# Router logits taken from the centred residual, and eleven cached pages loaded during the third tile of the time mixer

## The reference, cut to what matters

```
x = layer_norm(ALPHA * x + mixer(x), ln1_g, ln1_b)
lc = x @ moe_w_coarse + moe_b_coarse          # 4 groups
lf = x @ moe_w_fine[g] + moe_b_fine[g]        # 4 experts of each group
group = argmax(lc); two best experts of that group; weights by softmax
x = layer_norm(ALPHA * x + sum of the two experts, ln2_g, ln2_b)

layer_norm(x, g, b) = (x - mean) * rsqrt(var + 1e-5) * g + b
sample attention: softmax(q . cache_kv[page] + q_rope . cache_krope[page]) over 8 pages of 128 positions per sample
```

## Time and profile before

| what | value |
|---|---|
| three runs | 956.81, 960.07, 961.41 us, median 960.07 |
| profiled execution | 960.22 us, of which the span from the first to the last instruction is 958.5 |
| PE busy | 858.3 us, 90% of the span |
| DVE, ACT, POOL busy | 436.3, 244.0, 165.2 us |
| mean granted TensorE clock | 0.904 of full speed |
| DMA | 165.25 MB, 172 GB/s mean |

### The profile page before, as it was taken

The page is one execution under the profiler, slowest core; times in us unless marked ns, Lnnn a source line. Parts: engine busy times, 40 slices in busy tenths (PEclk is TensorE's granted clock), DMA queues, the critical chain, the costliest instruction groups (busy, mean ns, idle before and its releaser), DMA issues.

```text
span 958.5 us, 20599 instructions
## 1 busy us (share of the span) xinstructions
PE 858.3 (90%) x8552; PEld 616.0 (64%) x8552; DVE 436.3 (46%) x965; ACT 244.0 (25%) x532; POOL 165.2 (17%) x217
## 2 busy tenths in 40 slices
PE   5999998979999998999789889788978969999995
PEld 3787776757466656877655756558755747566653
DVE  3599754653124235148723343423634354042435
ACT  1135212051111113165235122130650060101013
POOL 5106041001400001000069630000810002300000
PEclk9999979998899999999999686865989988999997
DMA  9764802263999995421010220000826354999901
GB/s 263 258 176 75 162 12 94 89 234 102 413 417 416 418 307 159 132 75 63 1 19 4 90 79 4 2 1 3 252 89 220 132 224 166 417 417 417 415 36 46
DMA packets 79835, 165.25 MB, mean 172 GB/s; under 512 B 19809, under 2 KB 58136, under 8 KB 70850
## 3 DMA queue, kind: packets, MB, share of 16 engines
q1 hardware_dynamic: 68348, 149.43, 43.6%
q0 software_dynamic: 6624, 14.06, 4.9%
q10 hardware_dynamic: 4768, 0.41, 0.5%
HBM read 155.70 MB, written 6.99 MB: 170 GB/s over the span
## 4 chain that ended last, share of the span: by engine, by line
PE 76%; DVE 12%; issue 5%; ACT 2%; SPq 2%; DMA 2%; POOLq 0%; POOL 0%; DVEq 0%; ACTq 0%
PE bank L1666 12%; PE bank L2078 12%; PE bank L2110 7%; PE bank L1948 6%; PE bank L2122 5%; PE bank L816 3%; DVE scratch L2196 3%; PE bank L670 2%; SPq L2891 1%; PE bank L2067 1%; PE bank L694 1%; PE bank L2057 1%; DVE scratch L2193 1%; PE bank L2046 1%; PE bank L684 1%
## 5 line engine op out<-in xcount | busy, mean ns | idle before, releaser
L2651 ACT ACTIVATE scratch<-bank 128x280 f32<-128x280 f32 (+5 forms) x122 | 57.2, 476 | 415.9 <-PE bank L2110 114.2
L1666 PE MATMUL bank<-x_fm,weight_slots 128*128 128x280 f32 x576 | 142.7, 409 | 2.7 <-ACT x_fm L2742 1.3
L1666 PEld LDWEIGHTS bank<-x_fm,weight_slots 128*128 128x128 f32 x576 | 111.8, 195 | 31.5 <-issue 3.5
L2078 PE MATMUL bank<-weight_slots,scratch 128*64 128x256 f32 x672 | 92.5, 379 | 0.0
L2196 DVE TENSOR_TENSOR scratch<-bank,scratch 128x256 f32<-128x256 f32 x16 | 6.8, 425 | 157.4 <-PE bank L2078 157.4
L2078 PEld LDWEIGHTS bank<-weight_slots,scratch 128*64 128x64 f32 x672 | 58.6, 137 | 26.2 <-issue 4.6
L2122 PE MATMUL bank<-scratch 128*128 128x280 f32 x256 | 66.6, 406 | 0.0
L2196 DVE TENSOR_TENSOR scratch<-scratch 128x128 f32<-128x128 f32 (+14 forms) x76 | 50.8, 682 | 30.5 <-ACT scratch L2651 28.5
L1948 PE MATMUL bank<-scratch,weight_slots 128*128 128x280 f32 x256 | 62.6, 402 | 0.0
L1948 PEld LDWEIGHTS bank<-scratch,weight_slots 128*128 128x128 f32 x256 | 48.1, 190 | 13.7 <-issue 1.7
L2078 PE MATMUL bank<-scratch 128*64 128x256 f32 x352 | 56.9, 379 | 0.0
(11 more groups left out here) (441 smaller groups left out, 1308.6 us busy)
## 6 DMA issues: line engine op xcount, KB each, us to landing
weight_slots<-in_moe_w_down SPq DMA_DIRECT2D x24, 1024.0 KB, 12.6
weight_slots<-in_moe_w_up SPq DMA_DIRECT2D x22, 1024.0 KB, 10.7
weight_slots<-in_moe_w_gate SPq DMA_DIRECT2D x20, 1024.0 KB, 11.0
scratch<-in_moe_w_gate SPq DMA_DIRECT2D x12, 1024.0 KB, 9.9
scratch<-in_moe_w_up SPq DMA_DIRECT2D x10, 1024.0 KB, 10.7
weight_slots<-in_od_w_in SPq DMA_DIRECT2D x9, 1024.0 KB, 6.3
weight_slots<-in_ev_w_in SPq DMA_DIRECT2D x8, 1024.0 KB, 14.7
scratch<-in_moe_w_down SPq DMA_DIRECT2D x8, 1024.0 KB, 12.7
```

The lines of the kernel that those rows point to most:

```text
L1666: ins = pe.matmul(b[:, 0:NT], w[:, k, P * m2:P * m2 + P], src[:, k, :], start=(k == 0), stop=(k == kt - 1))
L2078: ins = pe.matmul(b[CAP * j:CAP * j + CAP, 0:DE], XG[:, q % 2, k, CAP * j:CAP * j + CAP], w[j][:, k, :], start=(k == 0), stop=(k == KD - 1))
L2651: return act.activation(dst, b[:rows, 0:width], f, **kw).then_inc(ring.free, 1)
```

## The change

Two things that don't touch each other, and a few small helpers.

First, the logits no longer come from the normed `XT`. With c the centred residual, s the scale of a token, g and b the norm's weight and bias and W the router's weights, x @ W = s * (c @ (g * W)) + b @ W. So the 16 x 20 columns of router weights are multiplied by `ln1_g` once, b @ W is added once to `RB`, both for both layers and ahead of layer 0's norm (on PE 32 one-column matmuls, counted as two per product by the profile, and two 20-column ones; on ACT three small activations and one copy; on DVE one multiply of 128x320 and one add of 128x40). In each layer the eight router matmuls now read `RES` right behind the squares, their bank is in ring A, ACT copies it to `LG4`, and DVE multiplies it by the spread scale ahead of the eight tiles of `RES`. The turn to token-major follows the scale. ACT now does all eight tiles of layer norm 1 (`ACT_TILES = (KD, 6)`; six still in layer norm 2), and all three `x_turned` come behind the logits, once all eight tiles of `XT` are there.

Second, of the 47 late pages, eleven have their homes in what the time mixer calls `ATF`, `KTF` and `BTF`, and these wait for `mark["rbk"]` of the third tile (DVE's last read of the products in which these tiles were used) in place of `y_free` = 3.

```diff
-EARLY_PAGES, READY_PAGES = 17, 56
+EARLY_PAGES, MIDDLE_PAGES, READY_PAGES = 17, 11, 56
-ACT_TILES = 6
+ACT_TILES = (KD, 6)
+        free_middle = [(16800 + 4 * 288, MIDDLE_PAGES)]
-        free_late = [(1024, 8), (5600, 11), (9248, 7), (16800, 16), (25152, 5)]
+        free_late = [(1024, 8), (5600, 11), (9248, 7), (16800, 4), (16800 + 15 * 288, 1), (25152, 5)]
...
                 if n == EARLY_PAGES:
...
+                    sp.wait_ge(*mark["rbk"])        # the same on POOL
+                if n == EARLY_PAGES + MIDDLE_PAGES:
                     sp.wait_ge(y_free, len(PT))
...
# PE, once, between hn_mean and hn_var; BC, BCB, RBX are new small tiles
+            for l in range(2):
+                for k in range(KD):
+                    g, w0 = 32 * (k % 4), 20 * (KD * l + k)
+                    ins = pe.matmul(b[g:g + 32, l:l + 1], RWF[:, w0:w0 + 32], vec("ln1_b", KD * l + k), start=(k < 4), stop=(k >= 4))
+            close(A, ins, "router_bias")
# behind hn_var
+            until("router_bias")
+                ins = pe.matmul(b[:, 20 * l:20 * l + 20], BCB[:, l, :], cst("sum4"), start=True, stop=True)
+            close(A, ins, "router_rows")
...
# PE, each layer
-                spread_scale(2 * l)
-                b = V.claim()
+                b = A.claim()
                 for k in range(KD):
-                    ln_tile(2 * l, k)
+                    if k < KD - 1:
+                        pe.wait_ge(ev("ln_centred"), (KD - 1) * 2 * l + k + 1)
+                    else:
+                        until(f"out{l}")
-                    ins = pe.matmul(b[g:g + 32, 0:NT], RWF[:, w0:w0 + 32], XT[:, k, :], start=(k < 4), stop=(k >= 4))
-                close(V, ins, f"lg{l}")
+                    ins = pe.matmul(b[g:g + 32, 0:NT], RWF[:, w0:w0 + 32], RES[:, k, :], start=(k < 4), stop=(k >= 4))
+                close(A, ins, f"lg{l}")
+                spread_scale(2 * l)
...
-                x_turned(0)
-                until(f"lg{l}")
+                pe.wait_ge(ev("lg_scaled"), l + 1)
                 # 3 small matmuls: sum4 of LG4
-                x_turned(1)
-                x_turned(2)
+                for k in range(KD):
+                    ln_tile(2 * l, k)
+                for t in range(3):
+                    x_turned(t)
...
# DVE, scaled(c)
                 b = V.take()
+                if c % 2 == 0:
+                    until(f"lg{c // 2}")
+                    s.mark(mul(LG4, LG4, b[:, 0:NT]), ev("lg_scaled"))
                 for m in range(KD):
                     s.mark(mul(RES[:, m, :], RES[:, m, :], b[:, 0:NT]), ev("ln_scaled"))
-                for m in range(ACT_TILES, KD):
+                for m in range(ACT_TILES[c % 2], KD):
...
# DVE, out_and_moe(l)
+                if l == 0:
+                    until("router_rows")
+                    s.do(mul(rw, rw, bc(vec("ln1_g", 0, 2 * KD), [P, 2 * KD, 20], 2)))
+                    s.do(add(RB[:, :, :], RB[:, :, :], RBX))
-                scaled(2 * l)
                 s.mark(dve.memset(PICK, 0.0), dve_step)
                 s.do(dve.memset(LG, 0.0))
-                s.do(dve.tensor_copy(LG4, b[:, 0:NT]), v_free)
+                scaled(2 * l)
...
# ACT, layer_norm, behind the root
+                if c % 2 == 0:
+                    empty(LG4, NT)
-                for m in range(ACT_TILES):
+                for m in range(ACT_TILES[c % 2]):
```

More of the change, by code:

```diff
@@ L367, in program @@
         MEANQ = part(5840, NT)
+        BC, BCB, RBX = part(4780, 2), part(4784, 2, P), part(5040, 2, 20)
         x_loads = [
@@ L440, in rows_landed, with tiles_of @@
             return 16 * sum((m, k) <= (l, q) for m in range(2) for k in range(1, NQ) if k % 4 == q % 4)
+        def tiles_of(c):
+            return sum(ACT_TILES[i % 2] for i in range(c))
         kt_read, score_banks = {}, {}
@@ L1897, in _ @@
             close(A, ins, "hn_var")
+            until("router_bias")
+            b = A.claim()
+            for l in range(2):
+                ins = pe.matmul(b[:, 20 * l:20 * l + 20], BCB[:, l, :], cst("sum4"), start=True, stop=True)
+            close(A, ins, "router_rows")
             def spread_norms():
                 pe.wait_ge(ev("norm_scale"), 1)
+                pe.wait_ge(a_free, A.n)
                 norms.extend((A.n, A.slot))
@@ L2212, in _ @@
             v2 = lambda r: r.rearrange("p (a b) -> p a b", a=2)
[L2213 removed]
+            s.do(mul(v2(t0), v2(are), dt), ev("angles"))
             s.do(mul(v2(t1), v2(aim), dt))
@@ L2720, in std @@
                     empty(sd[:, m, :], NT, ACT.Sqrt, scale=1.0 / n, bias=eps[e])
+            b = A.take()
+            s.do(act.activation(BC, b[:, 0:2], ACT.Copy))
+            s.do(act.activation(BCB[:, 0, :], cst("ones"), ACT.Identity, scale=BC[:, 0:1]))
+            act.activation(BCB[:, 1, :], cst("ones"), ACT.Identity, scale=BC[:, 1:2]).then_inc(a_free, 1)
             empty(OSD[:, 0, :], NT, ACT.Sqrt, scale=32.0 * 32.0 / RDV, bias=eps["32 1e-5"])
+            empty(RBX.rearrange("p l e -> p (l e)"), 40)
             for h in range(RH):
```

39 lines of the change are left out of this document (19 added, 20 removed).

## The result

| | before | after |
|---|---|---|
| median of the runs | 961.03 us (8 runs, 956.81 to 965.47) | 952.09 us (8 runs, 949.07 to 957.15) |
| profiled execution | 960.22, span 958.5 | 957.15, span 955.4 |
| mean granted clock in it | 0.904 | 0.896 |

After / before is 0.9919, with a 95% interval of 0.9891 to 0.9946: 7.8 us less, between 5.2 and 10.5 (the two medians lie 8.9 apart). The forecast was 953.4. The profiled execution of the changed kernel is the slowest of its eight, so the two profiles differ by 3.1 us only. They have to be compared stage by stage, not by their spans.

A forecast was written before the change was run, and what follows sets the result against it. TensorE, busy 90% of the span, was taken to bound the kernel through its work, gaps and clock. From 960.2, pages -6.0, router -1.2 and front +0.4 gave 953.4 us, range 949.2 to 957.3.

The forecast's parts named there:

- Part 1: Late pages of layer 1's mixer: eleven loaded during the third tile save 6.0 us, bounds 4.0 and 6.3.
- what is late next is ACT: After the third tile, PE next waits for ACT's exponentials, done at 704.5; the earlier start gains 4.0 us.
- I take 'stays': Clock stays up over PE's remaining 2.2 us wait before the probabilities' turns, bringing 2.0 us more.
- Rival (b): Clock falls in the 2.2 us wait left by ACT, router gives between nothing and 1.2: 956.0 us, chance 0.25.
- Rival (c): Pages do nothing, because something other than POOL's pace sets the last landing: 959.4 us, chance 0.06.
- Part 2: Router logits taken early in both layers' norm 1: 1.2 us saved over two layers, bounds 0 and 5.5.
- So I take half clock: After 4.0 us of idle PE, the router stage's 24 turns run at half clock, taking 5.2 us.
- ACT is not in the way: Router stage: ACT finishes its exponential and three small copies at 217.9, before `PLACE` wants them.
- 0.6 us of 0.9: Packing after the router: of 0.9 us earlier `PLACE`, 0.6 survives per layer, depending on when the clock returns.
- rival (d): The new 4.0 us gap holds the clock down past packing, 3.7 us lost per layer: 964.0 us, chance 0.05.
- Part 3: One-time router preparation ahead of layer 0's norm costs 0.4 us, bounds 0 and +1.5.
- The clock is full here: Ahead of layer 0's projection, full clock lets the two 20-column products cost only 0.4 us.

The follow-up runs named there:

- The router alone: Section on the change with all 47 pages late again, 958.28 us; its four: that, the change, and the change with idle products at the front or second weighing.
- pages_only: The kernel before plus only the eleven pages loaded in the third tile, old router kept: 956.02 us, ratio 0.9968.
- five_pages: The kernel before plus only five of the eleven pages loaded in the third tile, old router kept: 955.45 us, ratio 0.9954.
- orders_fed_two: both_orders plus three idle TensorE products ahead of the front's variance sums and three ahead of the second page weighing: 940.00 us, ratio 0.9812.
- both_orders: The change with ACT's three PICK copies ahead of its exponential and table load, and half the turns ahead of the second four tiles: 949.76 us, ratio 0.9885.

## Why the prediction came out right, point by point

**Part 1, the pages: right in mechanism, the size somewhat high.** The step "the wait goes entirely" and "what is late next is ACT" is what the earlier trace rows's counterpart shows: 2.13 us idle, released by the accumulation at L1483, where 2.2 was forecast. "I take 'stays'" was right for this gap in this profile (PEclk 1.00 from 707 to 712; 24 scores in 2.78 us). Rival (b)'s reason, that nothing on record keeps the clock over a gap of this length, had a counterexample in the prediction's own: 2.04 us, followed by 16 products in 4.04 us at a granted clock of 1.00. Between this pair of profiles the stage gave 5.87 us, forecast 6.0. On the means of all profiles it gave 4.5: the wait for the landing is 4.7 us in the two others that have it, and the clock stood at half behind it for 3.4 us there, not 6.8. So the 2.0 us which the forecast put on the clock were read off an execution in which it cost more than in the others. 4.5 is still within the bounds that the prediction gave. Rival (c) is out: the longest landing was 4.3 us and nobody waits for one.

**Part 2, the router: -1.2 was forecast, half in each layer. The means show 2.0 us gained in layer 0 up to the slots and nothing in layer 1.**
- The bias is added, and the routing walk on DVE starts, 2.7 us earlier after the root: right.
- "So I take half clock" for the turns was right for the start of them only. They took 4.40 us, not 5.2, as the clock came back inside them, at 214.6. "The counting of tokens ran at half already and still does" was wrong: it ran at full clock, and PE was done at 218.0, which is 216.0 with the 2.0 us of the later start taken off, against the 219.0 forecast. By the rule of the Trainium skill that the prediction cited (TensorE: Matmul & The Clock Gate, "Part 4: PE-mode transpose"), the fast clock doesn't engage in transposes. Here it came back after PE had done nothing but turns for 3.2 us and nothing at all for 4.0 us before them, and the kernel with idle products ahead of the turns ran all 24 at 1.00 in 2.78 us. The measurement decides: the rule doesn't hold for these float32 turns.
- "ACT is not in the way" was wrong, though ACT's own time was right. With the 2.0 us of the later start taken off, its copies end at 219.88 - 2.0 = 217.9, the number forecast; but as PE came earlier than forecast, ACT became the last. Putting the copies first moved `PLACE` by 1.5 and 1.8 us, which shows it. So `PLACE` gained 1.88 and 1.67, not 0.9.
- "0.6 us of 0.9" for the packing and what follows was the mis-sized step in layer 1. PE now idles before the packing for 3.7 us (1.88 before, at a clock that was at half anyway; both from layer 0). From `PLACE` to the slots the four profiles with the new router that are named under "The router alone" have 0.6 to 0.7 us more on the means than the four with the old one, from the slots to the end 1.3 more (162.0 to 162.3 against 160.7 to 160.8 us), and the expert loop's first 34 us stand at 0.85 in place of 0.90. That is the mechanism of rival (d), a clock held down past the packing, at less than half of its price: layer 1's net is 0, where -0.6 was forecast. In layer 0 the packing of the change ran 6.6 us at half in place of 3.5, but pages_only, with the old router, took 9.34 us there as well, and what happens behind the slots drowns in the 440 us stretch.

**Part 3, the front: the work was sized right, the clock was left out, and at 2.14 us the stage lies outside the bounds of 0 and +1.5.** The one-column products (32 by the profile's count) took 0.43 us inside the gap, and the small ones 0.62 against 0.4 forecast. The other 1.7 us of the 2.14 come from a clock that falls at about 167 and makes the projection's start 5.71 us in place of 4.02. "The clock is full here" was read off one profile of the kernel before, and another with the old router (five_pages) has the same fall. Idle products in the gap took 1.69 of the 2.14 away, at a clock of 1.00, which shows that it is the clock; the 0.45 that stays is the added work. Against the mean of the three profiles with the old router and the gap left empty (37.0 us) the front costs 1.6 us and not 2.14.

**The sum.** On the means of the stages the change is worth -4.5 (pages) - 2.0 (router, layer 0) + 0 (router, layer 1) + 1.6 (front) = -4.9 us, an estimate; from the one pair of profiles it is -5.9 + 2.1 - 0.5 + 0 = -4.3. The parts measured alone agree with the means: the pages 3.1 and 4.4 us, the router 1.2, and the product 0.9968 x 0.9988 = 0.9956 is 4.2 us. The change itself measured 7.8 us, with 5.2 as its lower end; by the intervals of the two parts I estimate that their product is good to about 4 us either way, so the two are not clear of each other. The forecast of -6.8 lies between, and its closeness owes something to chance: the pages and the front came out 1.5 and 1.2 us worse than forecast, the router 0.8 better. Where the other 3 us of the 7.8 come from, if they are more than noise, is not settled: no stage that the diff touches shows them, and the stretch of 440 us between varies by more than that from one execution to the next. Likewise open is why the two orders with two filled gaps gain 5 to 6 us more than the expected sum of their stages. That the clock stands at half for less of the time would fit both (the mean granted clock was 0.909 to 0.913 in all six runs of orders_fed_two, 0.900 to 0.903 in those of both_orders), but a profile shows one execution, of the others only the mean clock is known, and no run changes the middle stretch alone.

## What to carry to other kernels

A wait that is removed brings what lies between it and the next engine's readiness: find who is late next before you move more than is needed (five pages did nearly what eleven did). Take the length of a stage from several profiles: one pair gave the pages 5.9 us, the means 4.5. A dependency that is taken away early can leave PE idle later, and here a longer gap in front of the turns and the packing was followed by a lower clock, and in layer 1 all that the earlier start had gained was gone by the end, so the layer's time from a fixed landmark to its end is the number to look at, and not the landmark in between. Where PE has gaps of some 2 us amid light work, a few idle products on constants are a cheap trial: in two places, with an order that shortens the other gaps, they took the kernel with both orders from 0.9885 to 0.9812.

## What was not expected of the hardware

- The clock fell after a short gap with little work in it: the gap of the earlier trace rows (2.04 us), with 32 one-column products in it and 4 small ones behind it (the profile's count), was followed by a granted clock of 0.50 from 167 on (5.71 us for 16 products against 4.02), and the stage was as long in all seven profiles that had them with the gap left empty; without them it was 2.1 us shorter in two profiles of three, and the third had the fall (5.73 us).
- The same gap need not have the same effect each time: with 1.70 us without work ahead of the second weighing, the clock fell in its 64 products in five profiles of ten (5.35 us in place of 3.66 in the one shown), while behind a gap of 2.13 us ahead of the turns of the probabilities it stayed at 1.00 in the changed kernel.
- Float32 turns ran at full clock (24 in 2.78 us), and the clock rose while PE did nothing but turns, at 214.6.
- One table load of 1.28 us on ACT, in front of three copies of 0.23 us each, set the path of a whole stage: 1.5 and 1.8 us in two layers.
